# A hybrid-mixer MoE layer: stick-breaking scores and all attention outputs by pairs of heads

## What is computed

```python
proj = h @ w_in                      # (256, 5888): dilated q,k,v | stick-breaking q,k,v | gates A, B
# branch A: 12 heads of 64, three groups (window, dilation) = (128,1), (512,4), (2048,16)
scores = einsum('brnqhd,brnkhd->brnhqk', qs, kc) * hd ** -0.5      # after partial rotary of q and k
p = exp(where(valid, scores, -1e30) - max)
out = einsum('brnhqk,brnkhd->brnqhd', p, vc) / den     # the three groups merged by their denominators
# branch B: 8 stick-breaking heads of 64, strictly causal
z = einsum('bqhd,bkhd->bhqk', q_blk, kf) * hd ** -0.5
log_not = where(causal, -softplus(z), 0)
suffix = cumsum(log_not, axis=3, reverse=True) - log_not
weights = where(causal, exp(log_sigmoid(z) + suffix), 0)
out = einsum('bhqk,bkhd->bqhd', weights, vf)
# then
merged = sigmoid(ga) * (ya @ w_branch_a) + sigmoid(gb) * (yb @ w_branch_b)
x = x + gate1 * rms_norm(merged @ w_out)
# a mixture of 32 experts, top 4 of them for each token: clamped SwiGLU, w_up (1024x2048), w_down (1024x1024)
x = x + gate2 * rms_norm(moe_ffn(...))
```

## Time and profile before

| | |
|---|---|
| runs | 1356.35, 1356.79, 1361.42 us; median 1356.79 |
| profiled execution, its own time | 1359.0 us |
| its span, from the first to the last instruction | 1357.2 us |
| granted TensorE clock, mean | 0.948 |
| busy: TensorE, VectorE, ScalarE | 86%, 23%, 19% |
| moved by DMA | 464.89 MB, mean 343 GB/s |

### The profile page before, as it was taken

One profiled execution on the slowest core, in us unless ns is written; L12 is line 12 of the kernel. 1 busy time (PEld: TensorE's weight loads), 2 busy tenths in 40 slices (PEclk: granted clock), 3 DMA queues, 4 the chain that ended last, 5 costly groups with the idle time before them and its releaser, 6 DMA issues.

```text
span 1357.2 us, 21363 instructions
## 1 busy us (share of the span) xinstructions
PE 1173.1 (86%) x7951; PEld 585.8 (43%) x7952; DVE 311.6 (23%) x799; ACT 257.6 (19%) x389; POOL 0.2 (0%) x4
## 2 busy tenths in 40 slices
PE   4999899997998778989998989999978788787784
PEld 2845588855343325344244333342433233333332
DVE  1124534356111111212121111221211112111112
ACT  3034421213111211002112112021121111111211
POOL 0000000000000000000000000000000000000000
PEclk9899989998999987998999999999999889899898
DMA  9942384636589999658999999999999999999995
GB/s 334 381 176 93 106 309 164 228 126 247 214 305 417 418 417 416 232 183 351 417 417 419 418 412 417 417 417 419 417 418 417 419 417 417 417 418 419 418 417 238
DMA packets 102510, 464.89 MB, mean 343 GB/s; under 512 B 8172, under 2 KB 9540, under 8 KB 69574
## 3 DMA queue, kind: packets, MB, share of 16 engines
q1 hardware_dynamic: 100368, 461.52, 85.0%
q10 hardware_dynamic: 2102, 2.80, 0.6%
HBM read 463.24 MB, written 1.05 MB: 342 GB/s over the span
## 4 chain that ended last, share of the span: by engine, by line
PE 60%; DMA 22%; SPq 10%; DVE 4%; issue 3%; ACT 0%; DVEq 0%; ACTq 0%
PE psum L568 17%; PE psum L938 17%; DMA ring<-in_w_up 12%; PE psum L1011 10%; DMA ring<-in_w_down 8%; SPq L526 6%; PE psum L872 6%; SPq L521 4%; PE psum L930 3%; PE psum L1029 2%; DMA ring<-in_ada_w 1%; PE psum L574 1%; DVE area L1677 1%; PE psum L913 1%; PE psum L974 1%
## 5 line engine op out<-in xcount | busy, mean ns | idle before, releaser
L938 PE MATMUL psum<-ring,area 128*32 128x512 f32 (+2 forms) x2432 | 391.3, 622 | 50.4 <-DMA ring<-in_w_up 50.1
L938 PEld LDWEIGHTS psum<-ring,area 128*32 128x32 f32 (+2 forms) x2432 | 103.8, 121 | 331.9 <-issue 247.2
L1011 PE MATMUL psum<-ring,area 128*32 128x256 f32 (+2 forms) x2080 | 198.7, 422 | 24.8 <-DVE area L1662 14.8
L872 PEld LDWEIGHTS psum<-area 128*128 128x128 f32 x1056 | 130.7, 205 | 31.7 <-issue 31.7
L872 PE MATMUL psum<-area 128*128 128x128 f32 x1056 | 137.3, 291 | 0.3 <-DVE area L1568 0.3
L1011 PEld LDWEIGHTS psum<-ring,area 128*32 128x32 f32 (+2 forms) x2080 | 71.8, 114 | 141.2 <-issue 79.6
L1637 DVE TENSOR_SCALAR area<-psum 128x256 f32<-128x256 f32 x51 | 21.7, 425 | 388.9 <-PE psum L938 388.9
L1219 ACT ACT_TABLE_LOAD x32 | 41.1, 1283 | 350.4 <-PE psum L913 350.4
L1231 ACT ACTIVATE area<-area 128x256 f32<-128x256 f32 x51 | 21.3, 417 | 402.5 <-DVE area L1637 402.5
L568 PE MATMUL psum<-hT,ring 128*128 128x256 f32 x370 | 83.6, 386 | 0.0
L568 PE MATMUL psum<-ring,hT 128*128 128x512 f32 (+1 forms) x192 | 77.8, 561 | 0.0
(11 more groups left out here) (196 smaller groups left out, 672.8 us busy)
## 6 DMA issues: line engine op xcount, KB each, us to landing
ring<-in_w_up SPq DMA_DIRECT2D x256, 1024.0 KB, 18.9
ring<-in_w_down SPq DMA_DIRECT2D x128, 1024.0 KB, 22.2
ring<-in_ada_w SPq DMA_DIRECT2D x12, 2048.0 KB, 16.4
ring<-in_w_in SPq DMA_DIRECT2D x11, 2048.0 KB, 19.7
ring<-in_w_out SPq DMA_DIRECT2D x2, 2048.0 KB, 10.2
ring<-in_w_branch_b SPq DMA_DIRECT2D x1, 2048.0 KB, 9.6
cst<-in_cst ACTq DMA_DIRECT2D x1, 1184.5 KB, 7.9
x_res<-in_x SPq DMA_DIRECT2D x1, 1024.0 KB, 5.0
```

The source lines that it names most:

```text
L872: ins = pe.matmul(ps[banks[i]][:, kk % 4 * P:(kk % 4 + 1) * P], h2[:, tt, kk * P:(kk + 1) * P], S[:, tt, 0:P], start=(tt == 0 and kk % 4 = ...
L938: ins = pe.matmul(ps[b][g * P // G:(g + 1) * P // G, 0:w], XT[:, kk, t0:t0 + P // G], wt[:, c0:c0 + w], start=False, stop=kk == KT - 1, sk ...
L1011: ins = pe.matmul(ps[b][g * M:(g + 1) * M, 0:w], hidT[:, p, q * P + of * M:q * P + (of + 1) * M], down_weights(kk)[:, g * W + d * CW:g * W ...
```

## The change

The scores of stick-breaking are made for two heads at once, in the even iterations: first the 256-column matmul of head h and that of head h+1, then the two 128-column ones. Head h works on rows 0 to 63 of the array and head h+1 on rows 64 to 127, each into its own bank. The outputs of stick-breaking are made for two heads in the odd iterations, behind the sums, in turn for the two halves of the columns. So a head's weights have to be kept longer: `sb_weight` gives four places in place of two (two new ones in `xn`). The outputs of the dilated heads are made for slots i-1 and i together when i is odd; `dil_weight` gives the turned probabilities of an odd slot places of their own (in the dead part of `qk` and in `xn`). Because of that the broadcast of `gain1` moves behind the loop on ScalarE's queue.

The diff:

```diff
--- before.py
+++ after.py
@@ -258,7 +258,22 @@
         gates = region(10752, (16, T))
         sbw = region(10752, (10, TRI))
         prob = xn[:, 0:NG * P + NG * T]
+
+        def sb_weight(h):
+
+            if h % 4 < 2:
+                return sbw[:, 4 + h % 4, :]
+            return xn[:, NG * TRI + h % 2 * TRI:NG * TRI + (h % 2 + 1) * TRI]
+
         probT = region(8704, (NG, TRI))
+        probT2 = region(2048, (2, TRI))
+
+        def dil_weight(i, g):
+
+            if i % 2 == 0:
+                return probT[:, g, :]
+            return probT2[:, g, :] if g < 2 else xn[:, NG * TRI:NG * TRI + TRI]
+
         merged = region(5632, (KT, T))
         brw = region(7680, (4, T))
 
@@ -655,10 +670,16 @@
                 if h == 0:
                     for n in ("sbv0", "sbv1"):
                         un.wait_read(pe, n)
-                q, k = sb_head(h)
-                z = bank(f"z{h}")
-                fill(f"z{h}", [(z[:, 0:T], k[:, 0:P], q, True, True),
-                               (z[:, T:TRI], k[:, P:T], q[:, P:T], True, True)])
+                pair = (h, h + 1)
+                for i in pair:
+                    un.wait_free(pe, f"z{i}")
+                for lo, to, c0 in ((0, slice(0, T), 0), (P, slice(T, TRI), P)):
+                    for i in pair:
+                        q, k = sb_head(i)
+                        ins = pe.matmul(bank(f"z{i}")[:, to], k[:, lo:lo + P], q[:, c0:T], start=True, stop=True,
+                                        skip_group_check=True)
+                        if lo:
+                            ins.then_inc(bank_full[un.bank(f"z{i}")], 1)
 
             def sb_sums(h):
 
@@ -670,18 +691,17 @@
                                (c[:, T:TRI], tri_ge, sp_[:, T:TRI], True, True)])
 
             def sb_out(h):
-                pe.wait_ge(sb_w, h + 1)
-                w = sbw[:, 4 + h % 2, :]
-                v = [vtok[:, tt, DIL_W + h * HD:DIL_W + (h + 1) * HD] for tt in range(TT)]
+
                 name = f"sbo{h // 2}"
-                if h % 2 == 0:
-                    un.wait_free(pe, name)
-                o = bank(name)[h % 2 * HD:h % 2 * HD + HD, :]
-                pe.matmul(o[:, 0:T], v[0], w[:, 0:T], start=True, stop=False, skip_group_check=True)
-                ins = pe.matmul(o[:, P:T], v[1], w[:, T:TRI], start=False, stop=True, skip_group_check=True)
-                if h % 2:
-                    ins.then_inc(bank_full[un.bank(name)], 1)
-
+                un.wait_free(pe, name)
+                for tt, to, of in ((0, slice(0, T), slice(0, T)), (1, slice(P, T), slice(T, TRI))):
+                    for i in (h, h + 1):
+                        if tt == 0:
+                            pe.wait_ge(sb_w, i + 1)
+                        ins = pe.matmul(bank(name)[i % 2 * HD:i % 2 * HD + HD, to],
+                                        vtok[:, tt, DIL_W + i * HD:DIL_W + (i + 1) * HD], sb_weight(i)[:, of],
+                                        start=tt == 0, stop=tt == 1, skip_group_check=True)
+                ins.then_inc(bank_full[un.bank(name)], 1)
 
             dil = [("qk00", "qk0", 0), ("qk01", "qk0", 1), ("qk10", "qk1", 0), ("qk11", "qk1", 1),
                    ("qk20", "qk2", 0), ("qk21", "qk2", 1), ("va00", "va0", 0), ("va01", "va0", 1)]
@@ -694,12 +714,12 @@
                     g = arrived("va1")
                     w = chunk(g, DIL_W - CW)
                     fill("va1", tok_unit("va1", w, 0, DIL_W - CW) + tok_unit("va1", w, 1, DIL_W - CW, T))
-                if h < SB_H:
+                if h < SB_H and h % 2 == 0:
                     sb_scores(h)
                 if 1 <= h <= SB_H:
                     sb_sums(h - 1)
-                if h >= 2:
-                    sb_out(h - 2)
+                if h >= 3 and h % 2:
+                    sb_out(h - 3)
             pe.wait_ge(rot_done, 1)
             for u in range(6):
                 turn(f"qkT{u}", [(bank(f"qkT{u}")[:, i * T + tt * P:i * T + (tt + 1) * P],
@@ -738,19 +758,20 @@
                 gate_unit(2 * i + 1)
                 for g in range(NG):
                     un.wait_read(pe, f"pT{i}{g}")
+                if i % 2 == 0:
+                    continue
+
                 name = f"dlo{i // 2}"
-                if i % 2 == 0:
-                    un.wait_free(pe, name)
-                o = bank(name)[i % 2 * HD:i % 2 * HD + HD, :]
+                un.wait_free(pe, name)
                 for g in range(NG):
-                    h = g * SLOTS + i
-                    pe.matmul(o[:, 0:T], vtok[:, 0, h * HD:(h + 1) * HD], probT[:, g, 0:T],
-                              start=(g == 0), stop=False, skip_group_check=True)
-                    ins = pe.matmul(o[:, P:T], vtok[:, 1, h * HD:(h + 1) * HD], probT[:, g, T:TRI],
-                                    start=False, stop=(g == NG - 1), skip_group_check=True)
-                if i % 2:
-                    ins.then_inc(bank_full[un.bank(name)], 1)
-
+                    for tt, to, of in ((0, slice(0, T), slice(0, T)), (1, slice(P, T), slice(T, TRI))):
+                        for j in (i - 1, i):
+                            h = g * SLOTS + j
+                            ins = pe.matmul(bank(name)[j % 2 * HD:j % 2 * HD + HD, to],
+                                            vtok[:, tt, h * HD:(h + 1) * HD], dil_weight(j, g)[:, of],
+                                            start=(g == 0 and tt == 0), stop=(g == NG - 1 and tt == 1),
+                                            skip_group_check=True)
+                ins.then_inc(bank_full[un.bank(name)], 1)
 
             def spread(unit, rows_, half):
 
@@ -1101,7 +1122,7 @@
 
             def sb_weights(h):
                 act.wait_ge(sb_l, h + 1)
-                act.activation(sbw[:, 4 + h % 2, :], sbw[:, 8 + h % 2, :], ACT.Exp).then_inc(sb_w, 1)
+                act.activation(sb_weight(h), sbw[:, 8 + h % 2, :], ACT.Exp).then_inc(sb_w, 1)
 
             def sb_copy(p):
                 copy_out(f"sbo{p}", ybT[:, p * T:(p + 1) * T], ps[un.bank(f"sbo{p}")][:, 0:T])
@@ -1123,7 +1144,6 @@
                     sb_copy((h - 2) // 2)
             for u in range(6):
                 copy_out(f"qkT{u}", two(qkT[:, 2 * u:2 * u + 2, :]))
-            act.dma_start(gain1, a["norm_mix_post"][0:1, :].broadcast_to([P, D])).then_inc(ld_gain[0], 16)
 
             def gate_copy(n):
                 copy_out(f"g{n}", two(gates[:, 2 * n:2 * n + 2, :]))
@@ -1136,11 +1156,12 @@
                                accum_out=small[:, 29:30]).then_inc(dl_exp, 1)
                 gate_copy(2 * i)
                 for g in range(NG):
-                    copy_out(f"pT{i}{g}", probT[:, g, :], ps[un.bank(f"pT{i}{g}")][:, 0:TRI])
+                    copy_out(f"pT{i}{g}", dil_weight(i, g), ps[un.bank(f"pT{i}{g}")][:, 0:TRI])
                 gate_copy(2 * i + 1)
                 if i % 2:
                     p = i // 2
                     copy_out(f"dlo{p}", yaT[:, p * T:(p + 1) * T], ps[un.bank(f"dlo{p}")][:, 0:T])
+            act.dma_start(gain1, a["norm_mix_post"][0:1, :].broadcast_to([P, D])).then_inc(ld_gain[0], 16)
             act.dma_start(gain2, a["norm_ffn_post"][0:1, :].broadcast_to([P, D])).then_inc(ld_gain[1], 16)
             un.wait_read(act, "g7")
             for q in range(4):
```

## The result

| | before | after |
|---|---|---|
| runs beside each other, median | 1359.49 us (8 runs) | 1347.44 us (8 runs) |
| ratio of the two, 95% interval | | 0.9914, 0.9900 to 0.9929 |
| profiled execution, its own time | 1359.0 us | 1346.09 us |
| its span | 1357.2 us | 1344.2 us |
| mean granted clock | 0.948 | 0.950 |

One of the eight runs of the changed kernel took 2332.09 us at a granted clock of 1.00, which nothing here explains; it counts in the median and not in the ratio, and the other seven have a median of 1347.29.

What follows compares the result with a forecast made beforehand. TensorE was taken to bound the edited stages, DMA the experts' stage, which would start earlier as a whole. Gains of 3.4 + 2.3 + 4.1 = 9.8 us from the 1356.8 median gave 1347.0 us; 8-in-10 range 1343 to 1353.

Steps and rivals of the forecast that it cites:

- What bounds: Edited stages: TensorE sets the pace, so removed work moves all that follows, except just ahead of the 2.5 us wait.
- Rival (c): Expert stage or an idle gap takes the gain: 0 to 5 us gained, 1352 to 1357 us; chance 0.06.
- Pairs cost as one: Stick-breaking scores, its outputs and dilated outputs: a pair takes 0.86, 0.80 and 2.11 us, about one head's or slot's time.
- rival (a): Paired matmuls: halves overlap only in part, 1349.8 us without gain in 128-column steps, or 1351.9 with half the gain; chance 0.12.
- (b): Paired outputs: column pairs don't overlap their loads, 0.137 us each, giving 9.9 us back, 1356.9 us; chance 0.02.
- Only six heads' outputs count: End of stick-breaking: outputs of heads 6 and 7 hide in the rotation wait; the other six gain 2.3 us.
- Waits and moved work at zero: Edited stages: new waits, the moved gain broadcast and the gate weights' loads cost zero.
- The slack of an even head's sums: Stick-breaking loop: 8.1 us of cover for a chain of 5.4 leaves 2.7 us, so no wait for masked values.
- The sum of the loop: Stick-breaking loop: 3.4 us from scores and 2.3 from outputs, so the turns start 5.7 us earlier, near 163.8.
- Dilated outputs: Dilated heads: four outputs of 2.09 us become two pairs of 2.11, a gain of 4.1 us.
- Rival (d): Clock around the turns: six more low-clock stretches, 1.7 us each, make it slower than before, 1357 us and above; chance 0.02.
- The forecast's allowance of 1.7 us either way: Behind the wait ahead of the turns: one more or fewer stretch of 3.4 us at half clock shifts the result 1.7 us.

Runs made afterwards that it cites:

- by twos: Changed kernel with the dilated pair reordered: two matmuls of one slot, then two of the other; pair 2.16 us, run once at 1349.92 us.
- by fours: Changed kernel with the dilated pair reordered: four matmuls of one slot, four of the other, then two and two; pair 2.80 us, run once at 1351.01 us.
- by sixes: Changed kernel with each head's matmuls in a row in all pairs, six per dilated slot; dilated pair 3.45 us, median 1346.68 us, ratio 0.9920.

## Why the prediction was right, point by point

**What bounds.** Right. Removed work of TensorE moved all that follows, except in front of the wait for the rotation. The first read of a branch product came at 252.07 for 263.99 (forecast 254.2), the third expert's column pairs at 402.22 for 413.31 (forecast 403.5), the end of the span 13.0 earlier. SyncE's longest wait stayed that for the first expert matrix (189.9 us in 90 waits), and the DMA-bound stage took the same time or less. Rival (c) is out.

```profile
252.07 0.42 DVE L1474 TENSOR_TENSOR area<-psum,area 128x256 f32<-128x256 f32 x1 [16.85 <-PE psum L583]
...
402.22 13.90 PE L959 MATMUL psum<-ring,area 128*64 128x512 f32 x64
```

**Pairs cost as one.** Right in all three: 0.85, 0.80 and 2.10 for 0.86, 0.80 and 2.11. That includes the 128-column steps, for which the earlier trace rows had only quarters; rival (a) is out. The outputs settle (b) too: had column pairs not overlapped their loads, two slots would have taken 2.1 + 24 x 0.137 = 5.4 us by that rival's own price. The rule of the Trainium skill (TensorE: Matmul & The Clock Gate, The mechanism), that a load overlaps only where the row group differs, doesn't hold for the column halves here.

**Only six heads' outputs count.** Right: 6.22 and 6.21 us from the last sums to the turns, wait 2.52 both times.

**Waits and moved work at zero.** Right. TensorE waited for no masked values and no chunks, and for weights of stick-breaking only at the last pair, in the hidden stretch. The slack of an even head's sums, forecast at 2.7 us, was 2.4: the masked values of head 2 were ready at 108.91, and its sums started at 111.32.

```profile
108.42 0.49 DVE L1384 TENSOR_TENSOR area<-area,cst 128x128 f32<-128x128 f32 x2
```
The broadcast of the gain was issued at 242.25, behind the last dilated output, and took 7.7 us to land, before the first branch product was read at 252.07. From the gate row to the output projection it took 29.33 us before and after.

**The sum of the loop: the mis-sized term.** The turns came at 161.39 for a forecast of 163.8; 1.0 of that is an earlier start, the other 1.4 is that the loop gave 7.1 us and not 5.7. The prediction priced a change of shape as part of a score's 0.85 us and stopped there. It took from the order that scores and outputs now stand in different iterations, but didn't ask what the sums and the projection cost once they are neighbours. Both are matmuls on the whole array, and each is 0.1 us shorter for every side on which a half-array group no longer stands. Seven such groups left the loop (four of scores, three of outputs), with two sides each: 14 x 0.1 = 1.4 us, for which the sum had no term. The kernel with the sums first shows 1.19 us of this with no pairs at all, and the two loop edits by themselves give 4.15 and 2.95 where pairs alone give 3.4 and 2.3.

**Dilated outputs.** 4.1 was right (4.2 in the kernel with these alone, 2.1 for the half that lies where the clock was full). The profiled pair shows 3.8, since the execution after had 8.5 us of low clock in the stretch for 6.8.

**The clock.** Rival (d) needed six more stretches of 3.4 us at low clock. The prediction called that the whole stage at half clock, but it is some 20 of 84.5 us. In the edited stage the low time went from 6.8 to 8.5 us, half of one stretch. Nor did the edit leave TensorE idle for 0.8 us more ahead of the turns: the two waits went from 3.51 to 3.73 us, because the pair waits between its first matmul and its second. The forecast's allowance of 1.7 us either way is what two executions of one kernel differed by in an unedited stretch (29.33 and 30.97 us).

**Sum.** 7.1 + 4.1 = 11.2 us from the edited stages, in place of 9.8; the ratio says 11.7 (9.7 to 13.6). That 1347.0 met 1347.44 so closely owes something to luck, since two errors cancel: the forecast started from 1356.8, the median of three runs, which is 2.7 us below the 1359.49 of eight, and its gain was 2.3 us below the difference of the medians. What stays open is the expert stage: first to eighth expert took 265.7 to 266.2 us in three traces (the changed kernel twice, by twos), 268.0 to 268.4 in seven (the kernel before twice among them), and 266.9, 269.0 and 270.9 in the others. The kernel with one head behind the other has the same order of stages as the changed one and took 268.4, so no edit was found that it goes with.

## What to carry to other kernels

Work that uses half of the array is worth half only if a partner for the other half is near in TensorE's queue; group by pairs, and order the groups so that matmuls of the same shape become neighbours, since each change of shape has its own price. Before pricing an edit by its groups, read what the neighbours of each group become. And when an engine that runs ahead of a wait gets faster, look at the wait: here filling it with independent work gave 7 us, over half of what the pairing gave.

## What was not expected of the hardware

- Issue in turn isn't needed for two matmuls a head: head behind head, pairs of 256 and 128 columns took 0.86 and 0.81 us. With six matmuls a slot it is: 2.10 in turn, 2.16 by twos, 2.80 by fours, 3.45 by sixes.
- A group of matmuls on the whole array is 0.1 us longer for each side on which a group on half of the array stands: ahead of the change (7.06 for 6.97 us of projection) as well as behind it (1.08 for 0.97 us of sums). So a half-array group between two such groups costs 0.2 us on top of its own time. The Trainium skill, TensorEngine Tiling (Array Packing), Key Properties, says that a change of tiling mode drains TensorE; the rows fit that and give a price, which the page doesn't, but a drain itself is not seen in them. Between rows in halves and columns in halves (scores and then outputs, in the kernel with the sums first) no such price shows on top of the groups' own 0.85 and 0.79 us.
- Behind 3.5 to 3.7 us of idle TensorE ahead of the turns came 2.9 to 8.9 us at 1.2 GHz, in eleven traces; with the idle time filled, the clock was 1.00 over 70.55 us in both.
- The stretch from the gate row to the output projection, in which TensorE does the same in every kernel here, took 27.6, 29.3 or 31.0 us in the thirteen traces, with 0, 3.4 or 6.8 us at 1.2 GHz in it. That makes steps of 1.7 us between executions.
